# An expert's bias row brought to the partitions by DMA, in place of two selecting matmuls and a copy

## The reference

```python
def clamped_swiglu(h):
    glu, lin = h[..., ::2], h[..., 1::2]
    glu = jnp.minimum(glu, SWIGLU_LIMIT)
    lin = jnp.clip(lin, -SWIGLU_LIMIT, SWIGLU_LIMIT)
    return glu * jax.nn.sigmoid(SWIGLU_ALPHA * glu) * (lin + 1.0)

def expert_block(args):
    tok, gate, e = args
    hid = xt[tok] @ w1[e] + b1[e]          # 1024 -> 2048
    out = clamped_swiglu(hid) @ w2[e] + b2[e]   # 1024 -> 1024
    return out * gate[:, None].astype(out.dtype)
```

## Time and profile before

| what | us |
|---|---|
| median of 3 runs | 1564.85 |
| profiled execution | 1566.89 |
| its span, first to last instruction | 1565.1 |
| PE busy / DVE / ACT / GpSimd | 1513.3 / 759.4 / 538.8 / 360.2 |
| L1779, w1 units: 6144 matmuls | 667.3 busy |
| L1765, L1766, L1767, w2 units: 496 matmuls in each row | 200.8, 194.2, 194.8 busy |
| mean granted TensorE clock | 0.985 |

### The profile page before, as it was taken

The page is one execution under the profiler, slowest core; times in us unless marked ns, Lnnn a source line. Parts: engine busy times, 40 slices in busy tenths (PEclk is TensorE's granted clock), DMA queues, the critical chain, the costliest instruction groups (busy, mean ns, idle before and its releaser), DMA issues.

```text
span 1565.1 us, 28668 instructions
## 1 busy us (share of the span) xinstructions
PE 1513.3 (97%) x11426; PEld 874.0 (56%) x11426; DVE 759.4 (49%) x826; ACT 538.8 (34%) x622; POOL 360.2 (23%) x428
## 2 busy tenths in 40 slices
PE   9999999898998999999999999999999999999993
PEld 7777878785543544445554445554444554444552
DVE  5499866542535433444433444433344433344554
ACT  4534243310313332333333333333333333333343
POOL 5633552422230011211111211112111112121100
PEclk9999999999999999999999999999999999999997
DMA  5422111111468999999999999999999999999983
GB/s 172 168 84 76 31 21 56 52 59 31 188 256 307 365 387 379 391 387 391 392 396 382 388 386 390 389 396 379 384 393 383 394 393 386 382 391 383 410 335 124
DMA packets 96716, 456.19 MB, mean 291 GB/s; under 512 B 22913, under 2 KB 36903, under 8 KB 47502
## 3 DMA queue, kind: packets, MB, share of 16 engines
q1 hardware_dynamic: 86910, 434.49, 71.1%
q0 software_dynamic: 9600, 20.31, 5.4%
q10 hardware_dynamic: 144, 0.52, 0.1%
HBM read 442.89 MB, written 20.61 MB: 296 GB/s over the span
## 4 chain that ended last, share of the span: by engine, by line
PE 85%; DVE 10%; issue 2%; ACT 2%; DMA 1%; DVEq 0%; POOLq 0%; POOL 0%; ACTq 0%; SPq 0%
PE banks L1779 42%; PE banks L1765 8%; PE banks L1767 7%; PE banks L1766 7%; PE banks L1704 3%; PE banks L1796 1%; PE banks L1760 1%; PE banks L1492 1%; PE banks L1377 1%; PE banks L1378 1%; PE banks L1379 1%; PE banks L1772 1%; DVE AR L2052 1%; PE banks L1478 1%; PE banks L1557 1%
## 5 line engine op out<-in xcount | busy, mean ns | idle before, releaser
L1779 PE MATMUL banks<-slots,BK 128*32 128x512 f32 x6144 | 667.3, 593 | 0.0
L2121 DVE TENSOR_TENSOR lo<-slots,hi 128x2048 fp32r<-128x2048 f32 x128 | 293.1, 2293 | 376.5 <-ACT hi L1167 366.2
L1779 PEld LDWEIGHTS banks<-slots,BK 128*32 128x32 f32 x6144 | 195.7, 110 | 449.4 <-issue 449.1
L1167 ACT CAST hi<-slots 128x2048 fp32r<-128x2048 f32 x128 | 243.5, 1903 | 319.6 <-DMA slots<-in_expert_w_dram 312.1
L960 POOL DMA_INDIRECT x_sum<-hT,idy x32 | 47.0, 1468 | 689.4 <-issue 578.7
L1765 PE MATMUL banks<-lo,a_hi 128*128 128x512 f32 x496 | 200.8, 405 | 4.0 <-DVE lo L2121 4.0
L1767 PE MATMUL banks<-hi,a_lo 128*128 128x512 f32 x496 | 194.8, 393 | 0.0
L1766 PE MATMUL banks<-hi,a_hi 128*128 128x512 f32 x496 | 194.2, 392 | 0.0
L1765 PEld LDWEIGHTS banks<-lo,a_hi 128*128 128x128 f32 x496 | 93.6, 189 | 47.6 <-issue 23.3
L2310 DVE TENSOR_TENSOR a_lo<-banks,a_hi 128x768 fp32r<-128x768 f32 x31 | 29.7, 958 | 183.8 <-ACT a_hi L1252 183.8
L1767 PEld LDWEIGHTS banks<-hi,a_lo 128*128 128x128 f32 x496 | 93.7, 189 | 20.5
(11 more groups left out here) (401 smaller groups left out, 1616.4 us busy)
## 6 DMA issues: line engine op xcount, KB each, us to landing
slots<-in_expert_w_dram SPq DMA_DIRECT2D x384, 1024.0 KB, 8.2
slots<-in_w_in_dram SPq DMA_DIRECT2D x13, 1024.0 KB, 5.3
xs<-in_x_dram SPq DMA_DIRECT2D x8, 512.0 KB, 4.8
slots<-in_w_out_dram SPq DMA_DIRECT2D x2, 2048.0 KB, 9.0
x_sum<-slots POOLq DMA_DIRECT2D x1, 2560.0 KB, 11.5
h_rows<-slots SPq DMA_DIRECT2D x4, 512.0 KB, 2.6
slots<-x_sum SPq DMA_DIRECT2D x4, 512.0 KB, 5.0
out_dram<-hT SPq DMA_DIRECT2D x3, 512.0 KB, 2.6
```

What stands on the lines that cost most here:

```text
L1167: nc.scalar.copy(w2_hi[j][:, :, :], raw[n % RAW]).then_inc(hi_ready, 1)
L1779: ins = nc.tensor.matmul(bank[2 + g][j * CB:(j + 1) * CB, :], xT[q][:, k, g * CB:(g + 1) * CB], raw[n % RAW][:, j, :], start=(k == 0), sto ...
L2121: tensor_tensor(raw_lo[n % RAW][:, :, :], raw[n % RAW], w2_hi[j][:, :, :], ALU.subtract).then_inc(lo_ready, 1)
```

## The change

The table `b1` is no longer loaded as a whole, raised and split, and `sel`, `biases` and `keep_bias` are gone. For each block SyncE issues four DMAs (`load_bias`): DMA j reads the 512 words of column group j of `b1[e]` from DRAM 32 times and writes them to the partitions 32j to 32j+31, so 4 x 64 KB in rows of 2 KB. There are two such buffers, `bias_rows[q]` for even and odd blocks. Those of experts 0 and 1 are issued once at the point where the table was loaded; those of experts 2 to 31 in `next_units`, ahead of the load of w1 unit 4 of the same expert. In `swiglu` DVE waits for the bias's DMAs, adds 1.0 to the odd columns in place (128x256), waits for that, and then adds as before. GpSimd's wait for the split bias before its first gather is gone too.

```diff
+        bias_rows = [region(qk[:, :, :, :].rearrange("p a j t -> p (a j t)"), NG * CW + n * CW, CW) for n in range(2)]
+        def load_bias(eng, e, q):
+            for j in range(4):
+                eng.dma_start(bias_rows[q][j * CB:(j + 1) * CB, :],
+                              b1[0, bass.ds(e, 1), j * CW:(j + 1) * CW].to_broadcast([CB, CW])).then_inc(bias_loaded[q], 16)
...
-            for j in range(4):
-                sp.dma_start(biasrows[j * E:(j + 1) * E, :], b1[0, :, j * CW:(j + 1) * CW]).then_inc(bias_in, 16)
             for g in range(2):
                 for n in range(3):
-                    sp.dma_start(b2_half[g][n * E:(n + 1) * E], b2[0, :, g * CW:(g + 1) * CW]).then_inc(bias_in, 16)
+                    sp.dma_start(b2_half[g][n * E:(n + 1) * E], b2[0, :, g * CW:(g + 1) * CW]).then_inc(b2_in, 16)
+            for q in range(2):
+                load_bias(sp, q, q)
...
-            def next_units(i, q, e, e_before):
+            def next_units(i, q, e, e_before, bias=True):
                 for u in range(UNITS):
                     n = q * UNITS + u
                     wait_used(sp, i, n - RAW)
+                    if bias and u == 4:
+                        load_bias(sp, e, q)
                     if u < W1U:
                         load_w1(sp, e, u, n)
...
-            pool.wait_ge(bias_split, 2)
...
-                nc.scalar.copy(bias_row, bank[bias_bank][:, :]).then_inc(bias_kept, 1)
...
-            def biases(b, q):
-                pe.wait_ge(sel_set, b + 1)
-                for part in range(2):
-                    nc.tensor.matmul(bank[bias_bank][:, :], sel[:, q, :], b1r[:, part, :], start=(part == 0), stop=(part == 1))
...
             def block_work(i, q, overflow=False, last=False):
                 b = i * 2 + q
-                pe.wait_ge(bias_kept, b)
-                biases(b, q)
                 pe.wait_ge(hid_free, b)
...
-            def swiglu(i, b, n, first=False):
+            def swiglu(i, b, n, q, first=False):
+                dve.wait_ge(bias_loaded[q], i * 64 + 64)
+                tensor_scalar(bias_rows[q][:, 1:CW:2], bias_rows[q][:, 1:CW:2], 1.0, None, ALU.add).then_inc(bias_raised, 1)
                 wait_used(dve, i, n)
-                dve.wait_ge(bias_kept, b + 1)
-                tensor_tensor(inner, hid, bias_row.unsqueeze(1).to_broadcast([P, NG, CW]), ALU.add).then_inc(hid_free, 1)
+                dve.wait_ge(bias_raised, b + 1)
+                tensor_tensor(inner, hid, bias_rows[q].unsqueeze(1).to_broadcast([P, NG, CW]), ALU.add).then_inc(hid_free, 1)
...
-                set_expert(q, e)
                 act_low(b - 1)
```

More of the change, by code:

```diff
@@ L187, in hymba_layer @@
         last_hi, last_lo = (rounded(f"last_{nm}", "BK", BW, o, [P, FT, P]) for nm, o in (("hi", 3 * CW), ("lo", 3 * CW + KT * P)))
-        sel = rounded("sel", "BK", BW, 3 * CW + 2 * KT * P, [P, 2, P])
         a_hi = rounded("a_hi", "qk", BW, 3 * D, [P, FT, P])
         a_lo = rounded("a_lo", "hT", BW, 3 * D, [P, FT, P])
-        b1r = rounded("b1r", "qk", BW, 2 * D, [P, 2, CW])
         def halves_of(t):
@@ L319, in hymba_layer @@
         hid = banks[:, 2:2 + NG, :]
-        bias_bank = 2 + NG
+        spare_bank = 2 + NG
         y_banks = banks[0:NS, 6:8, :]
@@ L332, in hymba_layer @@
         g1_spread = sem("g1_spread")
-        bias_in = sem("bias_in")
+        b2_in = sem("b2_in")
+        bias_loaded = [sem(f"bias_loaded{q}") for q in range(2)]
         small_in = sem("small_in")
@@ L730, in next_units @@
                         load_w2(sp, e_before, u - W1U, n)
-            next_units(0, 1, 1, 0)
+            next_units(0, 1, 1, 0, bias=False)
             with sp.Fori(1, E // 2) as i:
@@ L747, in _ @@
                             wait_used(sp, i, n - RAW)
+                            if u == 4:
+                                load_bias(sp, e, q)
                             if u < W1U:
@@ L1205, in _ @@
                     if st == ("o", 2, 1):
+                        act.wait_ge(b2_in, 16 * 6)
                         for half in range(2):
                             nc.scalar.copy(b2r[half][:, :], b2_half[half]).then_inc(b2_split, 1)
-                    if st == ("o", 2, 0):
-                        act.wait_ge(bias_raised, 1)
-                        nc.scalar.copy(b1r[:, 0, :], biasrows).then_inc(bias_split, 1)
                     if st[2] == 1:
@@ L1276, in block_work @@
                 act_high(b - 1)
-                keep_bias(i, b, q * UNITS)
                 for j in range(W2U):
@@ L1284, in _ @@
             x_copy_first()
-            keep_bias(0, 0, FIRST, True)
             x_copy(1, 1)
@@ L1293, in _ @@
             act_high(0)
-            keep_bias(0, 1, UNITS)
             filled(act, "o", TT - 1, 1)
@@ L1855, in overflow_rows @@
                 pe.wait_ge(ovf_diag_ready, 1)
-                nc.tensor.matmul(bank[bias_bank][:, 0:2 * E], ones_b[0:E, :], ovf_diag[:, :, :].rearrange("p n e -> p (n e)"),
+                nc.tensor.matmul(bank[spare_bank][:, 0:2 * E], ones_b[0:E, :], ovf_diag[:, :, :].rearrange("p n e -> p (n e)"),
                                  start=True, stop=True).then_inc(ovf_full, 1)
@@ L2121, in low_part @@
                 tensor_tensor(raw_lo[n % RAW][:, :, :], raw[n % RAW], w2_hi[j][:, :, :], ALU.subtract).then_inc(lo_ready, 1)
[L2123 to L2126, removed]
             def take_positions(tt):
@@ L2162, in _ @@
             dve.wait_ge(consts_ready, 4)
-            step(nc.vector.tensor_reduce(expert_row[:, :], ident[:, :].rearrange("p (j e) -> p e j", j=4), AX, ALU.add))
-            step(nc.vector.tensor_reduce(row_block[:, :], ident[:, :].rearrange("p (j e) -> p j e", j=4), AX, ALU.add))
             tensor_tensor(rw[:, :, :], rw[:, :, :], vec("g2").unsqueeze(2).to_broadcast([P, KT, E]), ALU.mult).then_inc(rw_ready, 1)
@@ L2264, in _ @@
                         step(nc.vector.memset(a_hi[:, :, NS:].bitcast(f32), 0.0))
-                        set_expert(0, 0)
-                        set_expert(1, 1)
                     if st == ("o", 2, 1):
@@ L2324, in swiglu, with block_work @@
                 nc.vector.scalar_tensor_tensor(act, glu_t, GLU_TOP, lin_t, ALU.min, ALU.mult).then_inc(act_ready, 1)
-            def block_work(i, q, e, overflow=False):
+            def block_work(i, q, overflow=False):
                 b = i * 2 + q
-                set_expert(q, e)
                 act_low(b - 1)
@@ L2334, in block_work @@
                     low_part(i, W2U * (q - 1) + j, q * UNITS + W1U + j, j)
-                swiglu(i, b, q * UNITS + W1U - 1)
+                swiglu(i, b, q * UNITS + W1U - 1, q)
             def overflow_blocks():
@@ L2354, in overflow_tables @@
                 dve.wait_ge(ovf_full, 1)
-                ps = bank[bias_bank]
+                ps = bank[spare_bank]
                 step(nc.vector.tensor_copy(blkexp[:, :], ps[:, E:2 * E]))
@@ L2369, in _ @@
                 dense_gates(tt)
-            swiglu(0, 0, UNITS - 1, True)
+            swiglu(0, 0, UNITS - 1, 0, True)
             dve.wait_ge(gatesT_split, 1)
@@ L2381, in _ @@
                 low_part(0, j, UNITS + W1U + j, j)
-            swiglu(0, 1, UNITS + W1U - 1)
+            swiglu(0, 1, UNITS + W1U - 1, 1)
             for q in range(2):
-                block_work(1, q, 2 + q, q == 0)
+                block_work(1, q, q == 0)
             with dve.Fori(2, E // 2 - 1) as i:
                 for q in range(2):
-                    block_work(i, q, i * 2 + q)
+                    block_work(i, q)
             for q in range(2):
-                block_work(E // 2 - 1, q, E - 2 + q)
+                block_work(E // 2 - 1, q)
             for t in (last_hi, last_lo):
@@ L2401, in _ @@
                         b, n = i * 2 + q, W2U + q * UNITS
-                        e = dve.value_load(blkexp[0:1, bass.ds(i * 2 + (q - E), 1)], min_val=0, max_val=E - 1)
-                        set_expert(q, e)
-                        swiglu(i, b, n + W1U - 1)
+                        swiglu(i, b, n + W1U - 1, q)
                         for j in range(W2U):
```

22 lines of the change are left out of this document (removed).

## The result

The changed kernel takes 1641.8 us (median of three runs; 1639.91 to 1643.70), the kernel before 1564.89: a ratio of 1.0492, 95% interval 1.0474 to 1.0509, +76.9 us. A fourth run of the changed kernel took 2223.7 us at a mean granted clock of 0.646, where the others had 0.984, and isn't counted. I had forecast 1583 with a range of 1564 to 1595. The sign was right and the size wrong by a factor of four. The profiled execution took 1643.7 us, its span 1641.9 against 1565.1 before: the profile has +76.8 us to explain.

A forecast was written before the change was run, and what follows sets the result against it. PE and the DMA engines were taken as near-equal bounds, with DMA ruling after the change: 23.7 us of bias work less 5 won back and 0.5 earlier start, +18.2 us, forecast 1583 us, range 1564 to 1595.

The forecast's parts named there:

- PE's gain: Per block PE loses the two matmuls of L1772, 0.47 us (bounds 0.35 and 0.64), 14.6 us in all.
- That the DMA engines were nearly full: In the expert loop DMA needs 33.68 us a block against PE's pace of 33.77.
- Rival A: PE stays the bound in the loop and only its gain counts: 1550 us, chance 0.13.
- The price of the bias: Per block 128 more packets of 2 KB cost 0.79 us of DMA time, the middle of 0.65 and 0.93.
- The form of the sum: Loop's added DMA work less time won back and the earlier start: 23.7 - 5 - 0.5 = +18.2 us.
- the 5 us I let the loop win back: Holes in the loop's DMA time close in a longer queue: 0 to 10 us, taken as 5.
- PE waiting some 1 us per block ahead of L1796: Sign of a right forecast: in each block PE waits some 1 us for `swiglu` ahead of L1796.
- the slack of 4 us: On the w2 path the queue can grow by 4.7 us, four or five blocks, before PE waits.
- The parts at nothing: Work on DVE, ACT and SyncE and before the loop, such as DVE's +1.0 and SyncE's four issues: taken as nothing.
- B: Rival between: 0.7 to 1.0 us of DMA time free per block, 1559 to 1568 us, chance 0.07.
- C: Rival, slower: clock falls to half speed in each block, 1606 us, or 2 KB rows cost double, 1611; chance 0.07.

The follow-up runs named there:

- e1: The changed kernel without the bias DMAs inside the expert loop, only those of experts 0 and 1 issued: 1559.0 us, ratio 0.9957 to the kernel before.
- e5: The changed kernel with each bias row loaded once to four partitions (8 KB) and spread by a DVE shuffle: 1565.26 us, ratio 0.9995 to the kernel before.
- e2: The changed kernel with each bias fetch as one DMA writing the same 512 words to all 128 partitions: 1584.14 us, ratio 1.0125 to the kernel before.
- e3: The changed kernel with its four DMAs reading 32 different rows of the bias table instead of one row 32 times: 1643.16 us in one run.
- e7: The changed kernel with two DMAs of 64 neighbouring partitions in place of four of 32, same 128 packets: 1645.09 us in one run.
- e6: The changed kernel with only two of the four bias DMAs of each expert issued in the loop: 1610.69 us in one run.
- e4: The changed kernel with each of the four DMAs writing 32 partitions at a stride of 4 instead of 32 neighbours: 1584.5 us in one run.

## Why the prediction came out as it did

**PE's gain** was right. Forecast 0.47 us a block between bounds of 0.35 and 0.64; e1 shows 0.44 by the periods and 0.46 by the starts.

**That the DMA engines were nearly full** was right, and is the reading that carried the sign. I had 33.68 us of need against PE's 33.77, from landing times and their drift. e5, whose bias adds four packets, settles at 33.70; e1, with none, at 33.3 to 33.7 in its last blocks. The share of 1.00 at 388 GB/s was a full queue, and the higher rate of 421 in stretches was no reserve. Nor was 421 the highest, as I had called it; a window of the kernel before:

```profile
1120.00:1126.00 6.00, 6.00 (x48) 3.24 (x50) 0.96 (x1) 2.14 (x3) 1.65 (x2) 1.00 1.04 434
```

There the rate is 434 GB/s for 6 us, at a share that reads 1.04, and almost all packets are weight packets. Over a block, with its gathers and row additions, the same full engines give 388. The ceiling of about 435 GB/s that the Trainium skill, "Perfetto Trace Analysis", section Roofline, gives for a single core is thus reached here in a stretch of 6 us and never over a block. Rival A, which took the rate of such a stretch for the whole loop, would have made the kernel 15 us faster.

**The price of the bias** is the step that failed: "8 x 0.082 = 0.65", "0.93 us per block", "so I take the middle, 0.79". The bounds were for the bias's own packets, and even there the upper one was right: 2 KB packets took 116 ns in the loop after (mean of blocks 10 to 27), the price of the earlier trace rows, and 85 ns in e2, close to the 82 of the earlier trace rows. I should have seen why the two differed. The spread load of the earlier trace rows covers all 128 partitions; each 64 KB load of the earlier trace rows (L699) covers 32 neighbours. I explained the gap by the traffic beside the load and the length of its packets, and took the middle of two different things.

The larger part is no term of my sum at all: what the bias does to the weight packets beside it. Those of 8 KB took 327 ns in the mean before and 347 after. There are 96 of them per engine and block: 96 x 0.020 = 1.9 us. With the bias's own 8 x 0.116 = 0.93 that makes 2.8 us a block. Over the 26 blocks from 560 to 1500 us of after, bias packets run for 10.8 us in each, and the 8 KB packets that start meanwhile take 379 ns in the mean, against 334 outside; in e2 bias packets run for 6.7 us, and the 8 KB packets take 316 ns meanwhile against 330 outside. The means of blocks 10 to 27 sort all the kernels: 8 KB packets take 347 ns in after, e3 and e7, 340 in e6 with half the bias, and 326 to 328 in before, e1, e2, e4 and e5. DMA packets and the queue's share in such a stretch, 1049 to 1055 us of after:

```profile
DMA packets 356, 2.12 MB, mean 353 GB/s; under 512 B 57, under 2 KB 57, under 8 KB 111
...
q1 hardware_dynamic: 356, 2.12, 102.2%
```

and the same of e2, 1052 to 1058 us:

```profile
DMA packets 434, 2.55 MB, mean 426 GB/s; under 512 B 51, under 2 KB 51, under 8 KB 146
...
q1 hardware_dynamic: 434, 2.55, 103.3%
```

After: 102.2% of 16 x 6 us is 98.1 us; 111 - 57 = 54 packets of 2 KB at 0.116 take 6.3; the other 356 - 111 = 245, of 8 KB, take the remaining 91.8, 0.375 us each. In e2, 99.2 us less 95 x 0.085 leaves 91.1 for 288 packets, 0.316 each. (The small ones are counted at nothing in both.) The weight packets are a fifth longer while bias packets go to 32 neighbours at a time. Outside that stretch the changed kernel moves about as much as the others; its window at 1040 us:

```profile
1040.00:1046.00 6.00, 5.79 (x39) 3.83 (x32) 3.69 (x3) 3.94 (x3) 0.00 (x0) 1.00 1.01 419
```

**The form of the sum** held. Putting the measured price into it: 30 x 2.8 - 5 - 0.5 = +79 us, against +76.9. And it held where its premise did: for the same packets spread over the partitions, e2 and e4, forecast +18.2, measured +18.7 and +19.0. That close a hit has some luck in it. By the periods the bias costs e2 34.20 - 33.5 or 33.7 = 0.5 to 0.7 us and not 0.79, so that the 5 us I let the loop win back were too many by as much.

**How PE shows it.** "PE waiting some 1 us per block ahead of L1796" became 1.5 us (43.8 over 29 waits), and 35.7 us stood ahead of w2 units, 4.0 of them at the start of the loop as before. With 2.8 us a block instead of 0.8 the slack of 4 us was gone after two blocks instead of four or five, and later units ran late too. Landing took 14.6 us and not 11 to 13. The end followed the last w2 landing as it said: the transposes of block 31 come 75.9 us later, the span ends 76.8 later.

**The parts at nothing** stayed there. DVE's +1.0 (0.29 us, L2273) and the DMA waits on DVE stand on the path from landing to transposes, but the engines' share of 1.01 says that no load starts late for it. Of SyncE the same holds: four issues still take 1.8 us, and the queue covers them.

**The rivals.** A is excluded by e1, B with it. C had two mechanisms. Its first, a fall of the clock, didn't come: 1.00 through the loop, in spite of 1.4 us of idle PE per block. Its second, a price doubled beside a full weight queue, was the nearest in kind to what happened, but it was sized at 0.93 more where 1.9 was right, and shared a chance of 0.07 with the first. I gave no reason for it and so little weight. No row of before has a load to 32 or 64 neighbouring partitions beside the weights, but between the earlier trace rows stood a difference of 40% in price that asked for a reason.

**What stays open.** Shown is that the partitions which one DMA writes make the loss: e4 changes nothing else. How they do it is argued. The trace doesn't show which port or which of the 16 engines a packet uses. That packets collide at the ports is inferred from e2, e3, e4 and e7 and from the table in the Trainium skill, "SBUF — State Buffer", section "Door 1: The DMA port swizzle". A second reading may fit the same four runs, and e2's expectation touched it: what counts would be whether each engine writes the partitions that it writes in a weight load, and not how many ports a DMA reaches. No run here separates the two. Not settled either: why two of the four DMAs cost two thirds of the whole, and the 6 us between e5 and e1, of which the start is about 2 and the four extra packets are the likeliest rest.

## What to carry to other kernels

When a transfer is added beside a full DMA queue, price two things: its own packets, and what it does to the packets beside them; for the second, ask which partitions each single DMA writes. Slice a broadcast so that every DMA is spread over the partitions (all 128, or a stride of 4 instead of 32 neighbours), or fetch the row once and spread it on an engine that idles. Here the first would need another layout of the column groups, as e2 and e4 don't compute the reference; the second, e5, computes it and was level with the kernel before. And where two rows of a trace give two prices for packets of one size, find what differs between them before taking the middle.

## What the runs showed of the hardware

- A DMA of 64 KB to 32 neighbouring partitions, four times a block, lengthens the 8 KB weight packets from 327 to 347 ns in the mean of a block (23% of them over 350 ns instead of 8%) and the block by 2.8 us. Spread over the partitions with a stride of 4, the same bytes cost 0.5 to 0.7 us.
- In the loop a packet of 2 KB takes 116 ns when its DMA covers 32 neighbours and 85 ns when it covers all of the partitions (e2) or every fourth (e4).
- Reading one DRAM row 32 times in a DMA took no longer than reading 32 distinct rows (1641.8 us, e3 1643.16), and reading one row 128 times no longer than four rows 32 times each (e2 1584.14, e4 1584.5).
- A DMA share of 1.01 stood for 367 GB/s in after and for 391 in e2: the share tells that the engines are full, not how well they do.
- DVE's shuffle of 128x512 f32 within groups of 32 partitions took 0.75 us.
